# The first block's scan started ahead of the gate rows' end, with the weight remainders one level later on GpSimd

## The reference, cut to what matters

```python
def token_mixer(xn, w_in, b_in, ...):
    proj = xn @ w_in + b_in              # 1024 -> 4624 columns
    (h_q, h_f_fwd, h_f_bwd, h_i, h_g,    # HGRN2: 5 x 512 columns
     m_q, m_k, m_v, m_o,                 # mLSTM: 4 x 512 columns
     m_ig_fwd, m_ig_bwd, m_fg_fwd, m_fg_bwd) = split_cols(proj, IN_SPLITS)   # gates: 4 x 4
    q_h = to_heads(silu(h_q)); v_h = to_heads(h_i)
    lf_fwd = log_forget(h_f_fwd); lf_bwd = log_forget(h_f_bwd)
    o_h = hgrn2_scan(q_h, -expm1(lf_fwd), v_h, lf_fwd) + flip(hgrn2_scan(... backwards ...))
    ...

def hgrn2_scan(q, k, v, log_f):          # one step per chunk of tokens
    cum = cumsum(log_f)
    o_inter = (q * exp(cum)) @ state
    scores[t, s] = sum_d q[t, d] * k[s, d] * exp(cum[t, d] - cum[s, d])   for s <= t
    o = o_inter + scores @ v
    state = exp(cum_last) * state + (k * exp(cum_last - cum))^T @ v
```

## Time and profile before

| what | value |
|---|---|
| median of 3 runs | 1996.89 us (1995.45 to 1999.15) |
| the profiled execution: its time, its span | 1992.46 us, 1990.7 us |
| TensorE busy | 1902.8 us (96%), granted clock 0.996 |
| GpSimd busy | 998.0 us (50%) |
| VectorE busy | 781.1 us (39%) |
| ScalarE busy | 553.4 us (28%) |

### The profile page before, as it was taken

How to read it: one execution, slowest core, us unless ns; L and a number is a source line. 1 busy time by engine, 2 the same in 40 slices (tenths; PEclk the granted TensorE clock), 3 DMA queues, 4 the chain that set the end, 5 groups by cost and what they waited for, 6 DMA issues and landing times.

```text
span 1990.7 us, 23274 instructions
## 1 busy us (share of the span) xinstructions
PE 1902.8 (96%) x9434; PEld 1390.7 (70%) x9434; DVE 781.1 (39%) x1187; ACT 553.4 (28%) x1120; POOL 998.0 (50%) x568
## 2 busy tenths in 40 slices
PE   7999998999999999999989999999999999999988
PEld 6878887678788888888767768887854444434436
DVE  2455668561413301323545375554241221212124
ACT  4534438342412200211123442332230000000025
POOL 5796766657368877887555587446600000000012
PEclk9999999999999999999999999999999999999999
DMA  5321113322123223323322222212689999999982
GB/s 184 94 74 41 35 53 116 117 70 100 54 74 95 95 95 96 96 99 97 113 64 64 64 74 85 61 57 81 260 343 421 421 421 421 420 422 421 421 351 74
DMA packets 92697, 335.81 MB, mean 169 GB/s; under 512 B 7696, under 2 KB 9488, under 8 KB 67760
## 3 DMA queue, kind: packets, MB, share of 16 engines
q1 hardware_dynamic: 88864, 321.29, 43.2%
q10 hardware_dynamic: 3584, 12.52, 1.7%
q0 software_dynamic: 144, 0.52, 0.1%
HBM read 328.01 MB, written 6.29 MB: 168 GB/s over the span
## 4 chain that ended last, share of the span: by engine, by line
PE 78%; DMA 7%; POOL 6%; DVE 4%; ACT 3%; issue 1%; SPq 1%; PEldq 0%; ACTq 0%; DVEq 0%; PEld 0%; POOLq 0%
PE bank L609 48%; PE bank L1864 12%; DMA arena<-in_w_exp_up 3%; PE bank L1895 3%; POOL shared_r L667 2%; DMA shared<-in_w_exp_up 1%; DMA arena<-in_w_exp_gate 1%; DMA arena<-in_w_exp_down 1%; PE bank L786 1%; PE bank L630 1%; POOL shared_r L648 1%; POOL shared_r L649 1%; PE bank L1882 1%; PE bank L1068 1%; PE bank L1450 1%
## 5 line engine op out<-in xcount | busy, mean ns | idle before, releaser
L609 PE MATMUL bank<-shared_r 128*128 128x512 f32 (+1 forms) x3888 | 898.7, 387 | 18.0 <-POOL shared_r L667 7.3
L609 PEld LDWEIGHTS bank<-shared_r 128*128 128x128 f32 x3888 | 703.2, 189 | 174.4 <-issue 14.7
L648 POOL TENSOR_TENSOR shared_r<-shared,small 128x1024 fp32r<-128x1024 f32 (+1 forms) x172 | 335.3, 1949 | 847.9 <-DMA shared<-in_w_ple_gate 493.7
L649 POOL TENSOR_TENSOR shared_r<-shared,shared_r 128x1024 fp32r<-128x1024 f32 (+1 forms) x172 | 424.3, 2467 | 13.5
L1864 PE MATMUL bank<-arena 128*64 128x512 f32 x768 | 170.5, 595 | 9.8 <-DMA arena<-in_w_exp_up 3.8
L1864 PE MATMUL bank<-shared,arena 128*64 128x512 f32 x768 | 170.8, 594 | 9.4 <-DMA shared<-in_w_exp_gate 3.2
L609 PE MATMUL bank<-shared_r,arena_r 128*128 128x512 f32 x768 | 176.1, 391 | 0.0
L609 PEld LDWEIGHTS bank<-shared_r,arena_r 128*128 128x128 f32 x768 | 144.2, 188 | 31.6
L667 POOL TENSOR_TENSOR shared_r<-shared,shared_r 128x1024 fp32r<-128x1024 f32 x40 | 102.0, 2550 | 91.8 <-ACT shared_r L658 91.8
L1864 PEld LDWEIGHTS bank<-shared,arena 128*64 128x64 f32 x768 | 57.4, 137 | 116.9 <-issue 106.7
L1864 PEld LDWEIGHTS bank<-arena 128*64 128x64 f32 x768 | 56.0, 137 | 117.3 <-issue 103.3
(11 more groups left out here) (428 smaller groups left out, 2072.4 us busy)
## 6 DMA issues: line engine op xcount, KB each, us to landing
shared<-in_w_in SPq DMA_DIRECT2D x80, 512.0 KB, 3.6
arena<-in_w_exp_gate SPq DMA_DIRECT2D x32, 1024.0 KB, 25.5
shared<-in_w_exp_gate SPq DMA_DIRECT2D x32, 1024.0 KB, 25.8
shared<-in_w_exp_up SPq DMA_DIRECT2D x32, 1024.0 KB, 23.4
arena<-in_w_exp_up SPq DMA_DIRECT2D x32, 1024.0 KB, 24.2
arena<-in_w_exp_down SPq DMA_DIRECT2D x32, 1024.0 KB, 25.7
shared<-in_w_exp_down SPq DMA_DIRECT2D x32, 1024.0 KB, 26.1
shared<-in_w_up SPq DMA_DIRECT2D x32, 512.0 KB, 3.6
```

Of the source, the lines that this page charges most:

```text
L609: ins = pe.matmul(dst, W_, x_, start=first, stop=final)
L648: link(pool.tensor_tensor(hi, raw(p), small[:, 18:19].to_broadcast([P, hi.shape[1]]), ALU.add))
L649: pool.tensor_tensor(lo, raw(p), hi.bitcast(F32), ALU.subtract).then_inc(S_("w_split"), 1)
```

## The change

Nothing of the arithmetic changes; the order on three engines and one place in memory do.

- `HK` and `HST` swap places, so that `HK` no longer lies where the gate weights' pieces are.
- ScalarE writes the first halves of parts 0 and 1 of `proj_m` (after the first and the last of the four output gate operations); GpSimd's `early("proj_m")` goes, and GpSimd writes only their remainders.
- ScalarE and GpSimd no longer wait for the gate product ahead of the scan. ScalarE waits for it ahead of the first write to `HKD` (level 4 of chunk 0), GpSimd ahead of clearing `VM` (level 3 of chunk 0).
- On GpSimd each remainder comes one level later: after the differences of level l+1 instead of l. On ScalarE the first halves stay where they were.
- VectorE clears `HAT[0]` and the four `HKL` ahead of the output gate's additions, and multiplies the first two queries of chunk 0 ahead of storing `GZ`.

```diff
-    HKD, HK, HST = piece[0:3]
+    HKD, HST, HK = piece[0:3]
...
     def hg_act(act, hi):
-        bank_written(act, BASE["gz"])
         keys_of(0)
...
                     if i < ST - 1:
-                        if carried(m):
-                            bank_written(act, hg_bank["keys", carried(m)[-1], 0])
+                        bank_written(act, hg_bank["keys", carried(m)[-1], 0] if carried(m) else BASE["gz"])
...
     def hg_pool(pool, link):
-        lo = [2]
+        lo = [0]
...
         keys_sum(0)
-        bank_written(pool, BASE["gz"])
-        pool.memset(VM[:, :, :, C:CW], 1.0)
+        split_lo(pool, link, "proj_m", lo, 1)
         pool.wait_ge(S_("h_kl"), 1)
...
-                if l <= 4:
-                    split_lo(pool, link, "proj_m", lo, hg_parts(hg_steps(m, l)))
+                if 1 <= l <= 5:
+                    split_lo(pool, link, "proj_m", lo, hg_parts(hg_steps(m, l - 1)))
+                if l == 3 and m == 0:
+                    bank_written(pool, BASE["gz"])
+                    pool.memset(VM[:, :, :, C:CW], 1.0)
...
     def hg_dve(dve, link):
+        query(0, 0)
+        query(0, 1)
+        n = BASE["gz"]
+        bank = bank_take(dve, n)
+        bank_release(dve.tensor_scalar(GZ, bank[:, :], gbias, None, ALU.add), n)
         own_pairs(0)
...
     def _(pool):
-        early("proj_m")
         hg_pool(pool, link)
...
     def _(act):
+        hi = [0]
         for j in range(ST):
             bank_done(act, BASE["proj_h"] + 16 + j)
             act.activation(GATE[:, j, 0:512], GATE[:, j, 0:512], ACT.Silu)
+            if j in (0, ST - 1):
+                split_hi(act, "proj_m", hi, hi[0] + 1)
```

More of the change, by code:

```diff
@@ L674, in build @@
     HI = {}
-    for name in ("proj_h", "proj_m", "xk", "ple_gate"):
-        for p in [p for w in range(PB[name], next_stage(name)) for p in panels[w]["parts"]][2:]:
+    for name, first in (("proj_h", 2), ("proj_m", 0), ("xk", 2), ("ple_gate", 2)):
+        for p in [p for w in range(PB[name], next_stage(name)) for p in panels[w]["parts"]][first:]:
             HI[p] = len(HI) + 1
@@ L2506, in _ @@
             bank_release(dve.tensor_tensor(VH[:, j, :], bank[:, :], bc[:, 0:512], ALU.add), n)
+        link(dve.memset(HAT[0], 0.0))
+        for k in HKL:
+            last = dve.memset(k, 0.0)
+        last.then_inc(S_("h_kl"), 1)
         for j in range(ST):
```

20 lines of the change are left out of this document (6 added, 14 removed).

## The result

| what | before | after |
|---|---|---|
| median of the runs | 1996.17 us (1992.79 to 1999.15, 4 runs) | 1978.30 us (1978.27 to 1978.96, 4 runs) |
| the profiled execution: its time, its span | 1992.46 us, 1990.7 us | 1978.96 us, 1977.2 us |

The change makes the kernel faster: the ratio after to before is 0.9913, 95% interval 0.9901 to 0.9926. That is 17.9 us between the medians and 13.5 us between the two profiled executions. One of the eleven executions of the kernel with filled waits, further down, ran at a mean clock of 0.848 (2166.68 us) and is left out of the times given for it.

The account below looks back on a forecast made before the run. TensorE, busy 96% of the span, bounds the kernel; only its idle time can be won. Terms 2.17 - 1.1 + 2.27 + 2.45 + 2.9 - 0.7 = 8.0 us, giving 1989.0 us, range 1984 to 1997.

Parts of the forecast that it names:

- The start: Scan start, chunk 0: TensorE's 2.17 us wait at level 0 ends, less 1.1 us for a late `own`.
- the blocked case: Before `GZ`: GpSimd's second remainder blocks VectorE's query 1 until 136.5, so `own` starts 1.0 to 1.2 us late.
- Level 5 of chunks 1 and 5: TensorE's waits of 2.27 and 2.45 us there go, as level 5's differences no longer queue behind the remainder.
- Chunks 2 and 6: Level 0 waits of 0.86 and 0.87 us stay, the remainder still starting just ahead of the query.
- The seven small waits: Scan waits for queries behind a remainder and two differences, 2.9 us in all, go as differences come 1.2 us earlier.
- L818 and L1004: TensorE's waits for ScalarE's evacuation in chunk 2 (1.03 us) and VectorE's value bias (0.6 us) stay.
- New meetings: Eleven new places where a remainder meets a query cost 0.7 us in all; ends 0 and 16.5.
- all 13.1 us: Best end: all of TensorE's scan waits that shorter waits can give are gone, 1983.8 us.
- 4.4 us above that; I subtract the same 8.0: Step to the median: 1996.89 us lies 4.4 above the profiled execution; the same 8.0 us gain gives 1989.0.
- mostly given back: Rival: remainders meet the next level's queries, level 5 waits stay at half, small ones all stay; 1994.1 us, chance 0.18.
- only a shift: Rival: something hidden sets the scan's pace, the start's gain becomes a longer chunk 1 wait; 1996.4 us, chance 0.10.
- Slower: Rival: all eleven remainders block a query for 1.5 us, none covered, reaching TensorE; +7.8, 2004.7 us, chance 0.08.

Follow-up runs that it names:

- the kernel with filled waits: The kernel before, with two matmuls by zeros put ahead of each of TensorE's three longest scan waits; median 1994.83 us, ratio 0.9993.

## Why the prediction was wrong

The direction was right, and so was the mechanism of the largest terms; the start and chunks 2 and 6 were read wrong, the cost of a wait was too low, and the step from the profile to the median failed. By the steps of the sum:

- *The start, 1.1 of 2.17.* The step that failed is "I take the blocked case": query 1 began before the remainder and cost nothing, so the start gave 2.2. It led by 0.33 us. Of that, 0.21 is a difference that query 0 stretched (0.83 us instead of 0.62), so the lead was small but did not rest on the stretching alone. The rest is that the query came early: the forecast had it 2.1 us ahead of `own`'s start, and it came 2.6 ahead. A blocked query ahead of `GZ` was real only with the remainder a level earlier (0.32 us at `own`), and the bank was not worth a term of 1.0 to 1.2.
- *Level 5 of chunks 1 and 5, 2.27 and 2.45.* Right: no idle time there, and they stayed when only the start was changed.
- *Chunks 2 and 6, left at 0.86 and 0.87.* Wrong. The sentence "the remainder still starts just ahead of the query" failed: with the next pair ahead of it, the remainder comes 0.06 us behind the query, and the blocked query is one that TensorE does not need yet. With the old level back there, 1.16 and 1.28 us came back. The term was 1.73 us too low.
- *The seven small waits, 2.9.* Right but for 0.20 us that stayed (at 227.90). They were not all small: 1.18 of the 2.9 us is one wait, at level 0 of chunk 4, the same place as in chunks 2 and 6. That it would go was not argued for it by itself.
- *L818 and L1004, left at 1.03 and 0.6.* Right: 1.03 and 0.59 are there.
- *New meetings, -0.7.* None reached TensorE: 0.
- *What a wait costs.* Every term of the sum took a wait as its idle time. It costs some 0.2 us more on average, in matmuls that don't overlap: 2.6 us over the stretch, 0.24 for each of the 11 waits, and 0.19 a wait when 48 were added. With two waits brought back it was nearly nothing. No term of the sum had this.

Put together: 8.0 + 1.1 + 1.73 + 0.7 - 0.2 + 2.6 = 13.9 us, against 14.0 in the stretch, and 13.5 in the profiled span with its later `own`. I had called "all 13.1 us" the best end; it was no end, since it was a sum of idle times.

The medians moved by 4.4 us more than the profiles. The step that failed is "4.4 us above that; I subtract the same 8.0". The 4.4 us between the profiled execution and the median were not an offset of both kernels: the changed kernel has no such distance (1978.30 against 1978.96). What fits is falls of the clock behind the long waits, which the profiled execution happened not to have in the scan, and which went with the waits. In the one execution of before with three such falls the stretch was 4.2 us longer; the scan of every profiled kernel without a wait of about 2 us reads 1.00 (the changed kernel twice and seven others, whose longest wait was 1.28). The fall does not always come: the kernel with the remainders alone moved waited 2.17 us and its stretch reads 1.00 too. The test that should have settled it, the kernel before with its long waits shortened, took away the slowest executions but was worth 1.4 us (between 3.2 gained and 0.4 lost), where 2.5 to 4.5 was expected. So that these falls are a part of the 4.4 us is supported, that they are all of it is not shown, and where the rest lies stays open.

Of the signs named, level 0 at 137.72, level 5 without idle time and later stages unchanged in their sum (1692.7 us) came true; GpSimd's waits inside the scan, 32.1 - 9.6 = 22.5 us, met the 22; TensorE idle at 5 to 6 us did not (1.99).

The rivals: "mostly given back" and "only a shift" both fell with the waits gone. "Slower" needed six blocked queries to reach TensorE; at most one did, by 0.20 us.

## What to carry to other kernels

When a wait of the bounding engine goes, count its idle time and an allowance for the overlap around it, and do not take the sum of idle times as the best case. When the median lies well above the profiled execution, look at the granted clock of the runs before carrying the difference over: it may in part be a cost of the waits that the change removes. And where two engines exclude each other, which of them starts first can turn on 0.1 us, so price both outcomes in the range, but move the work by a whole step if it has to be safe.

## What the hardware showed that I had not expected

- 48 short waits of TensorE between its own matmuls cost 11.8 us, 0.25 each: 0.05 is seen as idle time, and 0.19 appears as longer busy time (clock 1.00 throughout). Two longer waits that were brought back added next to nothing to the busy time (0.03 us).
- In some executions the granted clock falls to about half (0.51 to 0.57 over windows of 3 to 7 us) behind a wait of 1.98 to 2.46 us between dense work; in other executions of the same program it does not. In the scan no wait of up to 1.28 us was followed by one. Behind the scan that does not hold: in the changed kernel the clock fell shortly after 307 us, where TensorE's waits had been only 0.88 and 0.67 us:

```profile
305.12 1.81 PE L562 MATMUL bank<-ident,arena 128*128 128x128 f32 x8 [0.88 <-ACT arena L1104]
307.61 1.97 PE L562 MATMUL bank<-ident,arena 128*128 128x128 f32 x8 [0.67 <-DVE shared_r L707]
```

```profile
307.50:310.50 3.00, 2.89 (x14) 2.69 (x15) 2.88 (x8) 2.38 (x6) 1.22 (x1) 0.50 0.17 60
```

- 48 added short waits did not lower the clock: 0.995 to 0.997 over its runs.
